# Loads of v paced by the planes of the running convolution, and an F32 context projection from unsplit weights

## Chip, cores and metric

The kernel runs on one core of one Trainium2 chip. The metric is the device time of one execution in microseconds (us), from the first to the last instruction and what lies around it; less is better.

## What is computed

One layer with two mixers that read the same normalised and modulated input: a chunked Mamba-2 scan in both directions, and an order-2 long convolution. Both matter here only in part. The first matter is the context prefix of 256 tokens, of which only the columns `m_xbc` (2048) and `m_dt` (32) of the input projection are wanted:

```python
h = rmsnorm(x, norm_w) * (1.0 + scale[:, None]) + shift[:, None]
hc = rmsnorm(ctx, norm_w) * (1.0 + scale_c) + shift_c
cols = in_projection(h, w_in, ALL_IN_NAMES)
cols_c = in_projection(hc, w_in, ("m_xbc", "m_dt"))
```

The second is the long convolution, order by order:

```python
u = depthwise_conv_centred(proj, conv_w, conv_b)
v, x1, x2 = jnp.split(u, 3, axis=-1)
z = v
for o, gate in enumerate((x1, x2)):
    z = gate * (bidir_long_conv(z, filt[:, 0, o], filt[:, 1, o]) + h_bias[o] * z)
```

Everything is float32. D_MODEL is 1024, SEQ 2048, CTX_LEN 256.

## The kernel before

The program is a row of phases, one block of instructions per engine each, with a barrier of all engines between them: modulation and filter network (`phase_modulation`), normalisation of the latent input together with the context projection (`phase_norm`), the input projection (`phase_in_projection`, the longest), filter taps, filter spectra, long convolutions (`phase_long_convs`), three phases of the scan, and the merge with the output projection. Each engine runs its own instructions in the order written; semaphores tie the engines together.

**`phase_norm`** (buffers `nl_...`). The 1024 channels are 8 tiles of 128 (KT). VectorE scales a piece of the input into PSUM (`scaled`, L435), ScalarE adds the shift and rounds to the high part (`high`, L389), VectorE makes the low part (`low`, L442). First come 8 pieces of the context (256 columns, `nl_c_hi` and `nl_c_lo`), then 32 pieces of the latent input (512 columns, `hl_hi` and `hl_lo`). Beside the 32 pieces run 17 tiles of weights of the context projection (16 of `m_xbc`, one of `m_dt`), two pieces to a tile. A tile of weights (128x1024, 512 KB) is loaded by SyncE (L324) into one of two slots, rounded to a high part by ScalarE (L396), its low part is made by GpSimd (L357), and TensorE then makes 24 matmuls of 256 columns (L370 to L372: high by high, high by low, low by high for each of 8 k). ScalarE evicts the result (L414), VectorE runs a three-tap convolution on it (`conv`, L451, L453, L456), ScalarE applies SiLU (L402), and SyncE stores it (L332). VectorE's order in an iteration n is: two pieces (scaled, low, scaled, low), then `conv(n - 1)`. ScalarE's is: eviction of tile n, rounding of weights n + 2, two `high`, SiLU of n - 1. A rounded tile is an `F32R` matmul operand, a plain one an `F32` operand; the `F32` matmuls of the long convolutions are the second kind.

**`phase_long_convs`** (buffers `conv_...`). The 1024 channels are four blocks of 256, each with two orders, so eight convolutions j in the order (block, order) = (0,0) (1,0) (0,1) (1,1) (2,0) (3,0) (2,1) (3,1). Convolution j has a stage of 16 steps q (`first` of j at L1005, `turn` and `last` of j - 1 at L1017 and L1027, the gate of j - 1 on VectorE at L1110), and then a stage of 32 planes (NPL): TensorE's `forward` (L1039), VectorE's product with the filter's spectrum (L1134, counted by the semaphore `s_p`), TensorE's two matmuls of `inverse` (L1049, L1050). SyncE loads the spectra, 512 KB for two planes, into four slots (SLOT, L948 and L950): the load of a slot waits until the two planes four slots earlier are multiplied. GpSimd's queue brings everything else by four 512 KB chunks each: v of a block (`load_x`, L960, into `x[:, blk % 2]`), the gate inputs of convolution j (`load_gate`, L967, three slots), and the stores of finished blocks (L979). GpSimd issues in program order: v of blocks 0 and 1 at the start; the gates of each convolution; and after the stores of block 0 (in j = 2) and block 1 (in j = 3) a wait for them to land, v of block 2 or 3, and the next gates.

Of the kernel before, what the change touches and what calls it, by code (L numbers as in the profile page):

```python
# [16 lines left out]
F32 = mybir.dt.float32  # L17
# [265 lines left out]
def phase_norm(nc, t, keep, rs, h_hi, h_lo, xbc_c, dt_c):  # L283
# [3 lines left out]
    with ExitStack() as ctx:  # L287
        ph = Phase(nc, "nl", ctx)
        c_hi, c_lo = ph.sb("c_hi", [P, KT, CTX], F32R), ph.sb("c_lo", [P, KT, CTX], F32R)
        x = ph.sb("x", [P, 4, 2, 512])  # L290
        w = ph.sb("w", [P, 2, D])
        w_hi, w_lo = ph.sb("w_hi", [P, 2, D], F32R), ph.sb("w_lo", [P, 2, D], F32R)
# [7 lines left out]
        s_w, s_whi, s_wlo, s_mm = ph.sems("w", 2), ph.sem("whi"), ph.sem("wlo"), ph.sem("mm")  # L300
# [11 lines left out]
        @block.sync  # L312
        def _(sp):
            def load_x(n):
                b, k, wd = piece(n)
                if n >= 4:
                    sp.wait_ge(s_xn, 2 * (n - 4) + 2)
                src = cv[:, k:k + 2, :] if b < 0 else xv[:, k:k + 2, b * 512:(b + 1) * 512]
                sp.dma_start(x[:, n % 4, :, 0:wd], src).then_inc(s_x[n % 4], 16)

            def load_w(n):
                if n >= 2:
                    sp.wait_ge(s_wlo, n - 1)
                sp.dma_start(w[:, n % 2, :], t["w_rec"][T_XBC + n]).then_inc(s_w[n % 2], 16)  # L324

            def store(n):
                if n < 2 * KT:
                    sp.wait_ge(s_res, n + 1)
                else:
                    sp.wait_ge(s_ev, NW)  # L330
                dst = xbc_c[n * P:(n + 1) * P, :] if n < 2 * KT else dt_c
                sp.dma_start(dst, res[:, n % 2, :]).then_inc(s_st[n % 2], 16)  # L332

            for n in range(4):
                load_x(n)
            sp.dma_start(taps[:], t["conv_taps"]).then_inc(s_taps, 16)
            load_w(0)
            load_w(1)
            nx = 4
            for n in range(NW):  # L340
                while nx < NX and nx < n + 8:
                    load_x(nx)
                    nx += 1
                if n + 2 < NW:
                    load_w(n + 2)
                if n >= 2:
                    store(n - 2)
            store(NW - 2)
            store(NW - 1)
            for q in range(2):  # L350
                sp.wait_ge(s_st[q], 16 * ((NW + 1 - q) // 2))

        @block.gpsimd
        def _(pool):
            for n in range(NW):
                pool.wait_ge(s_whi, n + 1)
                nc.gpsimd.tensor_tensor(w_lo[:, n % 2, :], w[:, n % 2, :], w_hi[:, n % 2, :].bitcast(F32),  # L357
                                        ALU.subtract).then_inc(s_wlo, 1)

        @block.tensor  # L360
        def _(pe):
            pe.wait_ge(s_lo, KT)
            for n in range(NW):
                pe.wait_ge(s_wlo, n + 1)
                if n >= 2:
                    pe.wait_ge(s_ev, n - 1)
                out = bank[n % 2][:, 0:CTX]
                for k in range(KT):
                    m = slice(k * P, (k + 1) * P)
                    pe.matmul(out, w_hi[:, n % 2, m], c_hi[:, k, :], start=(k == 0), stop=False)  # L370
                    pe.matmul(out, w_hi[:, n % 2, m], c_lo[:, k, :], start=False, stop=False)
                    mm = pe.matmul(out, w_lo[:, n % 2, m], c_hi[:, k, :], start=False, stop=(k == KT - 1))  # L372
                mm.then_inc(s_mm, 1)

        def place(n):

            b, k, wd = piece(n // 2)
            k += n % 2
            v = 1 if b < 0 else 0
            at = slice(0, CTX) if b < 0 else slice(b * 512, (b + 1) * 512)  # L380
            hi, lo = (c_hi, c_lo) if b < 0 else (h_hi, h_lo)
            return v, k, wd, hi[:, k, at], lo[:, k, at]

        @block.scalar
        def _(act):
# [6 lines left out]
            def weights(n):  # L392
                act.wait_ge(s_w[n % 2], 16 * (n // 2 + 1))
                if n >= 2:
                    act.wait_ge(s_mm, n - 1)
                nc.scalar.activation(w_hi[:, n % 2, :], w[:, n % 2, :], ACT.Copy).then_inc(s_whi, 1)  # L396

# [6 lines left out]
            for n in range(KT):  # L404
                high(n)
                if n in (4, 6):
                    weights(n // 2 - 2)
            done = KT
            for n in range(NW):
# [8 lines left out]
                if n + 2 < NW:  # L418
                    weights(n + 2)
# [8 lines left out]
        def _(dve):  # L428
            def scaled(n):
                v, k, wd, hi, lo = place(n)  # L430
                dve.wait_ge(s_x[n // 2 % 4], 16 * (n // 8 + 1))
                if n >= 2:
                    dve.wait_ge(s_lo, n - 1)
# [28 lines left out]
            scaled(0)  # L462
            for n in range(1, KT):
                scaled(n)
                low(n - 1)
            low(KT - 1)
# [13 lines left out]
            dve.wait_ge(s_lo, 2 * NX)  # L480
# [428 lines left out]
def phase_long_convs(nc, tables, u_s, z2_s, spec_s):  # L909

    NQ, NR, SLOT = 16, 8, 4
    with ExitStack() as ctx:
# [45 lines left out]
        def _(pool):  # L958
# [11 lines left out]
            for blk in range(2):  # L970
                for c in range(4):
                    load_x(blk, c)
            for j, (blk, o) in enumerate(convs):
                if o == 1:
# [6 lines left out]
                    if blk < 2:  # L981
                        pool.wait_ge(s_st, 64 * (blk + 1))
                        for c in range(4):
                            load_x(blk + 2, c)
# [1200 lines left out]
```

## Time and profile before

| What | us |
|---|---|
| Median of three runs | 4069.07 |
| Lowest and highest of them | 4060.92, 4069.66 |
| The profiled execution | 4071.49 |
| Span in its trace | 4069.7 |
| PE busy in the span | 3687.1 (91%) |
| DVE, ACT, POOL busy | 1726.3 (42%), 1215.7 (30%), 1023.3 (25%) |

All times in the trace are us from the start of the span of that one execution. PE is TensorE, DVE VectorE, ACT ScalarE, POOL GpSimd, SP SyncE; PEclk is the granted TensorE clock, 1.00 being 2.4 GHz and 0.50 being 1.2 GHz. An `F32` matmul is recorded as two matmuls, so a row of one `F32` matmul reads x2. An "idle before" in square brackets names what ended it. "q0 software_dynamic" is GpSimd's DMA queue, "q1" SyncE's.

### The profile page before, as it was taken

The numbers are of one execution on the slowest core, as the hardware profiler recorded it, in microseconds if no ns is written. First come the engines' busy times: TensorE is split into PE (matmuls) and PEld (weight loads), VectorE is DVE, ScalarE is ACT, GpSimd is POOL, SyncE is SP. The second block draws the span as 40 slices with busy tenths as digits, with TensorE's granted clock in tenths as the row PEclk, the third lists the DMA queues.
The fourth block names the chain that finished last, engine by engine and source line by source line (L and its number), as shares of the span: only waits on it lengthen the run. The fifth ranks groups of instructions, "written<-read, shape, count | busy, mean of one in ns | idle before, by whom it ended". The sixth has DMA issues, their size and how long they took to land. (4 is left out here: it accounts for less than half of the span.)

```text
span 4069.7 us, 44722 instructions
## 1 busy us (share of the span) xinstructions
PE 3687.1 (91%) x17082; PEld 2998.7 (74%) x17082; DVE 1726.3 (42%) x2050; ACT 1215.7 (30%) x2356; POOL 1023.3 (25%) x482
## 2 busy tenths in 40 slices
PE   5599999999999999996799899899766888799998
PEld 2578888888888888884599677677644777588886
DVE  5724430001433430003644454455367766566662
ACT  3411111111111011112377454455302554333332
POOL 0321112122222222111000101101047664344443
PEclk8899999999999999997899999999878999899999
DMA  6423322121211112116999757755667344555662
GB/s 250 159 86 119 114 96 77 62 77 62 77 62 77 67 72 77 62 67 246 306 301 275 179 135 165 166 130 125 157 241 275 125 156 135 209 190 194 207 191 101
DMA packets 386935, 597.40 MB, mean 147 GB/s; under 512 B 152019, under 2 KB 238979, under 8 KB 374395
## 3 DMA queue, kind: packets, MB, share of 16 engines
q1 hardware_dynamic: 297229, 403.94, 32.8%
q10 hardware_dynamic: 80336, 157.83, 10.1%
q0 software_dynamic: 9216, 33.56, 3.6%
q8 instruction: 99, 1.62, 0.2%
q14 instruction: 55, 0.45, 0.0%
HBM read 392.22 MB, written 203.03 MB: 146 GB/s over the span
## 5 line engine op out<-in xcount | busy, mean ns | idle before, releaser
L599 PE MATMUL pl_bank<-hl_hi,pl_w_hi 128*128 128x512 f32 x2336 | 923.7, 395 | 17.5 <-POOL pl_w_lo L570 17.5
L600 PE MATMUL pl_bank<-hl_lo,pl_w_hi 128*128 128x512 f32 x2336 | 922.6, 395 | 0.0
L601 PE MATMUL pl_bank<-hl_hi,pl_w_lo 128*128 128x512 f32 x2336 | 922.3, 395 | 0.0
L599 PEld LDWEIGHTS pl_bank<-hl_hi,pl_w_hi 128*128 128x128 f32 x2336 | 440.7, 189 | 120.0 <-issue 17.6
L601 PEld LDWEIGHTS pl_bank<-hl_hi,pl_w_lo 128*128 128x128 f32 x2336 | 440.7, 189 | 102.9
L600 PEld LDWEIGHTS pl_bank<-hl_lo,pl_w_hi 128*128 128x128 f32 x2336 | 440.7, 189 | 102.2
L567 POOL TENSOR_TENSOR pl_w_hi<-pl_w,pl_zero 128x1024 fp32r<-128x1024 f32 x73 | 138.1, 1892 | 1280.4 <-PE pl_bank L601 1275.7
L675 DVE TENSOR_SCALAR pl_res<-pl_raw,pl_taps 128x2048 f32<-128x2048 f32 x40 | 84.4, 2109 | 777.8 <-ACT pl_raw L625 777.8
L1775 PE MATMUL mo_bank<-mo_hi,mo_w_hi 128*128 128x512 f32 x768 | 305.5, 398 | 23.6 <-POOL mo_w_lo L1747 18.3
L1747 POOL TENSOR_TENSOR mo_w_lo<-mo_w,mo_w_hi 128x1024 fp32r<-128x1024 f32 x96 | 237.6, 2476 | 277.5 <-ACT mo_w_hi L1818 277.5
L1777 PE MATMUL mo_bank<-mo_hi,mo_w_lo 128*128 128x512 f32 x768 | 300.5, 391 | 0.0
L1776 PE MATMUL mo_bank<-mo_lo,mo_w_hi 128*128 128x512 f32 x768 | 300.4, 391 | 0.0
L625 ACT ACTIVATE pl_raw<-pl_bank 128x512 f32<-128x512 f32 x160 | 92.8, 598 | 664.3 <-PE pl_bank L601 430.0
L625 ACT ACTIVATE pl_res<-pl_bank 128x512 f32<-128x512 f32 x132 | 78.7, 598 | 617.8 <-PE pl_bank L601 617.2
L1134 DVE TENSOR_TENSOR conv_prod<-conv_bank,conv_spec 128x512 f32<-128x512 f32 x256 | 174.0, 690 | 179.9 <-PE conv_bank L1039 134.3
L1098 ACT COPY conv_v<-conv_bank 128x256 f32<-128x256 f32 x256 | 154.0, 602 | 243.2 <-PE conv_bank L1050 243.2
L570 POOL TENSOR_TENSOR pl_w_lo<-pl_w,pl_w_hi 128x1024 fp32r<-128x1024 f32 x73 | 199.3, 2730 | 5.8
L1775 PEld LDWEIGHTS mo_bank<-mo_hi,mo_w_hi 128*128 128x128 f32 x768 | 144.9, 189 | 59.1 <-issue 18.4
L1049 PE MATMUL conv_bank<-conv_prod,tab_wi 128*128 128x256 f32 x512 | 159.5, 394 | 24.4 <-DVE conv_prod L1134 23.7
L1776 PEld LDWEIGHTS mo_bank<-mo_lo,mo_w_hi 128*128 128x128 f32 x768 | 145.0, 189 | 30.9 <-issue 1.9
L1777 PEld LDWEIGHTS mo_bank<-mo_hi,mo_w_lo 128*128 128x128 f32 x768 | 145.0, 189 | 30.5
L967 POOL DMA_DIRECT2D conv_gin<-u_s x32 | 36.7, 1150 | 518.8 <-DVE conv_x L1110 512.0
(212 smaller groups left out, 5896.1 us busy)
## 6 DMA issues: line engine op xcount, KB each, us to landing
conv_spec<-spec_s SPq DMA_DIRECT2D x248, 256.0 KB, 4.9
mo_w<-in_w_br SPq DMA_DIRECT2D x96, 512.0 KB, 3.9
pl_w<-in_w_rec SPq DMA_DIRECT2D x73, 512.0 KB, 3.3
kern_s<-taps_res SPq DMA_DIRECT2D x16, 2048.0 KB, 7.0
spec_xin<-kern_s SPq DMA_DIRECT2D x64, 512.0 KB, 5.6
spec_s<-spec_res ACTq DMA_DIRECT2D x128, 256.0 KB, 4.1
st_xb<-tok_s SPq DMA_DIRECT2D x36, 768.0 KB, 7.0
u_s<-pl_res ACTq DMA_DIRECT2D x24, 1024.0 KB, 3.9
```

Of the source, the lines that this page charges most:

```text
L570: nc.gpsimd.tensor_tensor(w_lo[:, q, :], w[:, q, 0:D], w_hi[:, q, :].bitcast(F32), ALU.subtract).then_inc(s_lo, 1)
L599: pe.matmul(out, w_hi[:, q, m], h_hi[:, k, r], start=(k == 0), stop=False)
L600: pe.matmul(out, w_hi[:, q, m], h_lo[:, k, r], start=False, stop=False)
L601: mm = pe.matmul(out, w_lo[:, q, m], h_hi[:, k, r], start=False, stop=(k == KT - 1))
L625: nc.scalar.activation(dst, bank[b][:, 0:BW], func).then_inc(s_ev, 1)
L1049: pe.matmul(out, wi[:, k, :], prod[:, n % 4, 0, :], start=True, stop=False)
L1098: nc.scalar.copy(v[:, :, k], bank[2 + k % 2][:, 0:CB]).then_inc(s_vm, 1)
L1134: nc.vector.tensor_tensor(prod[:, n % 4], bank[ubank[k % 4]][:, None, 0:CB].to_broadcast([P, 2, CB]), spec[:, n // 2 % SLOT, :, k % 2], AL ...
L1747: nc.gpsimd.tensor_tensor(w_lo[:, s % 3, :], w[:, s % 3, :], w_hi[:, s % 3, :].bitcast(F32), ALU.subtract).then_inc(s_wlo, 1)
L1775: pe.matmul(bank[s % 4][:], w_hi[:, q, m], hi[:, slot, k, :], start=(k == 0), stop=False)
L1776: pe.matmul(bank[s % 4][:], w_hi[:, q, m], lo[:, slot, k, :], start=False, stop=False)
L1777: mm = pe.matmul(bank[s % 4][:], w_lo[:, q, m], hi[:, slot, k, :], start=False, stop=(k == KT - 1))
```

## The change

In `phase_norm` the context is kept as one F32 buffer `c` in place of `c_hi` and `c_lo`, and the weights are used as loaded: `w_hi` and `w_lo` go, `w` has four slots in place of two. The 24 F32R matmuls of a tile become 8 F32 matmuls. ScalarE's 17 roundings (L396), GpSimd's 17 subtractions (L357) and VectorE's 8 low parts of the context are gone. A tile's weights are loaded when the matmuls of four tiles earlier are done. The first group of matmuls waits for each piece of the context in turn and not for all eight. In `phase_long_convs`, v of block 1 is no longer loaded at the start but chunk by chunk during convolution 0, when its planes 4, 12, 20 and 28 are multiplied; v of blocks 2 and 3 are loaded likewise during convolutions 3 and 4. The number of bytes is the same.

```diff
@@ phase_norm
-        c_hi, c_lo = ph.sb("c_hi", [P, KT, CTX], F32R), ph.sb("c_lo", [P, KT, CTX], F32R)
+        c = ph.sb("c", [P, KT, CTX])
-        w = ph.sb("w", [P, 2, D])
-        w_hi, w_lo = ph.sb("w_hi", [P, 2, D], F32R), ph.sb("w_lo", [P, 2, D], F32R)
+        w = ph.sb("w", [P, 4, D])
...
             def load_w(n):
-                if n >= 2:
-                    sp.wait_ge(s_wlo, n - 1)
-                sp.dma_start(w[:, n % 2, :], t["w_rec"][T_XBC + n]).then_inc(s_w[n % 2], 16)
+                if n >= 4:
+                    sp.wait_ge(s_mm, n - 3)
+                sp.dma_start(w[:, n % 4, :], t["w_rec"][T_XBC + n]).then_inc(s_w[n % 4], 16)
...
-        @block.gpsimd
-        def _(pool):
-            for n in range(NW):
-                pool.wait_ge(s_whi, n + 1)
-                nc.gpsimd.tensor_tensor(w_lo[:, n % 2, :], w[:, n % 2, :], w_hi[:, n % 2, :].bitcast(F32),
-                                        ALU.subtract).then_inc(s_wlo, 1)
-
         @block.tensor
         def _(pe):
-            pe.wait_ge(s_lo, KT)
             for n in range(NW):
-                pe.wait_ge(s_wlo, n + 1)
+                pe.wait_ge(s_w[n % 4], 16 * (n // 4 + 1))
                 if n >= 2:
                     pe.wait_ge(s_ev, n - 1)
                 out = bank[n % 2][:, 0:CTX]
                 for k in range(KT):
-                    m = slice(k * P, (k + 1) * P)
-                    pe.matmul(out, w_hi[:, n % 2, m], c_hi[:, k, :], start=(k == 0), stop=False)
-                    pe.matmul(out, w_hi[:, n % 2, m], c_lo[:, k, :], start=False, stop=False)
-                    mm = pe.matmul(out, w_lo[:, n % 2, m], c_hi[:, k, :], start=False, stop=(k == KT - 1))
+                    if n == 0:
+                        pe.wait_ge(s_hi, k + 1)
+                    mm = pe.matmul(out, w[:, n % 4, k * P:(k + 1) * P], c[:, k, :], start=(k == 0), stop=(k == KT - 1))
                 mm.then_inc(s_mm, 1)
...
@@ phase_norm, VectorE
-            scaled(0)
-            for n in range(1, KT):
+            for n in range(KT):
                 scaled(n)
-                low(n - 1)
-            low(KT - 1)
@@ phase_long_convs, GpSimd's queue
-            for blk in range(2):
+            def load_paced(j, blk):
                 for c in range(4):
+                    pool.wait_ge(s_p, NPL * j + 8 * c + 4)
                     load_x(blk, c)
+
+            for c in range(4):
+                load_x(0, c)
             for j, (blk, o) in enumerate(convs):
+                if j == 0:
+                    load_paced(0, 1)
                 if o == 1:
                     for c in range(4):
                         load_gate(j, c)
...
                     if blk < 2:
                         pool.wait_ge(s_st, 64 * (blk + 1))
-                        for c in range(4):
-                            load_x(blk + 2, c)
+                        load_paced(j + 1, blk + 2)
```

GpSimd's queue in the long convolutions, from the start to the v of block 2. A wait is shown by the name under which the semaphore was first allocated: `ada_root` is the count of finished gates, `ada_rstd` that of stores, `ada_x1` that of planes, `s_p`; `z_s` is the buffer of finished blocks. Before:

```order
L960 DMA conv_x<-u_s 128x16x64 x8
L967 DMA conv_gin<-u_s 128x16x64 x3
L967 DMA conv_gin<-u_s 128x16x64 [waits ada_root] x9
L979 DMA z_s<-conv_x 128x16x64 [waits ada_root] x4
L960 DMA conv_x<-u_s 128x16x64 [waits ada_rstd]
L960 DMA conv_x<-u_s 128x16x64 x3
L967 DMA conv_gin<-u_s 128x16x64 [waits ada_root] x4
```

After:

```order
L940 DMA conv_x<-u_s 128x16x64 x4
L940 DMA conv_x<-u_s 128x16x64 [waits ada_x1] x4
L947 DMA conv_gin<-u_s 128x16x64 x3
L947 DMA conv_gin<-u_s 128x16x64 [waits ada_root] x9
L965 DMA z_s<-conv_x 128x16x64 [waits ada_root] x4
L940 DMA conv_x<-u_s 128x16x64 [waits ada_x1,ada_rstd]
L940 DMA conv_x<-u_s 128x16x64 [waits ada_x1] x3
L947 DMA conv_gin<-u_s 128x16x64 [waits ada_root] x4
```

Nothing is reordered, but each chunk of v of blocks 1, 2 and 3 now waits for planes, and the first gates behind it wait with it.

SyncE's queue at the start of `phase_norm` (`nl_x` pieces of context and latent input, `nl_w` weights, `nl_taps` convolution taps, `xbc_c` the result). Before:

```order
L336 DMA nl_taps<-in_conv_taps 128x160
L324 DMA nl_w<-in_w_rec 128x1024 x2
L319 DMA nl_x<-in_xT 128x2x512 x4
L324 DMA nl_w<-in_w_rec 128x1024
L319 DMA nl_x<-in_xT 128x2x512
L324 DMA nl_w<-in_w_rec 128x1024
```

After:

```order
L335 DMA nl_taps<-in_conv_taps 128x160
L323 DMA nl_w<-in_w_rec 128x1024 x4
L318 DMA nl_x<-in_xT 128x2x512 x5
L323 DMA nl_w<-in_w_rec 128x1024
L318 DMA nl_x<-in_xT 128x2x512
L323 DMA nl_w<-in_w_rec 128x1024
```

Two more tiles of weights (1 MB) go ahead of the first latent pieces.

ScalarE in `phase_norm`, from the first eviction on. Before:

```order
L414 ACTIVATE nl_raw<-nl_bank 128x256
L396 ACTIVATE nl_w_hi<-nl_w 128x1024
L389 ACTIVATE hl_hi<-nl_xn,keep_mod 128x512 x2
L414 ACTIVATE nl_raw<-nl_bank 128x256
L396 ACTIVATE nl_w_hi<-nl_w 128x1024
L389 ACTIVATE hl_hi<-nl_xn,keep_mod 128x512 x2
```

After:

```order
L397 ACTIVATE nl_raw<-nl_bank 128x256
L380 ACTIVATE hl_hi<-nl_xn,keep_mod 128x512 x2
L397 ACTIVATE nl_raw<-nl_bank 128x256
L380 ACTIVATE hl_hi<-nl_xn,keep_mod 128x512 x2
```

The rounding that stood between an eviction and the two `high` is gone, and with it its wait for the weights. VectorE's order in the latent part is unchanged.

## Rows read from the trace of the kernel before

**Rows 1.** Waits in `phase_norm`, 88 to 205: us in total, times, longest

```profile
PE nl_bank L370 <- POOL nl_w_lo L357: 29.5, 13, 4.3
DVE hl_lo L442 <- ACT hl_hi L389: 17.5, 11, 5.7
```

**Rows 2.** Timeline of `phase_norm`: start, duration, engine, line, what

```profile
90.67 1.06 ACT L396 ACTIVATE nl_w_hi<-nl_w 128x1024 fp32r<-128x1024 f32 x1 [1.80 <-DMA nl_w<-in_w_rec]
...
103.42 0.38 ACT L414 ACTIVATE nl_raw<-nl_bank 128x256 f32<-128x256 f32 x1 [0.38 <-PE nl_bank L372]
...
107.94 0.48 DVE L456 SCALAR_TENSOR_TENSOR nl_acc<-nl_raw,nl_taps,nl_acc 128x256 f32<-128x256 f32 x1
...
184.45 2.37 POOL L357 TENSOR_TENSOR nl_w_lo<-nl_w,nl_w_hi 128x1024 fp32r<-128x1024 f32 x1 [2.94 <-ACT nl_w_hi L396]
...
185.65 1.33 DVE L451 TENSOR_SCALAR nl_acc<-nl_raw,nl_taps 128x256 f32<-128x256 f32 x1
...
187.93 0.75 DVE L435 SCALAR_TENSOR_TENSOR nl_xn<-nl_x,keep_mod,rs_rows 128x512 f32<-128x512 f32 x1
...
190.77 0.40 DVE L451 TENSOR_SCALAR nl_acc<-nl_raw,nl_taps 128x256 f32<-128x256 f32 x1
...
192.13 0.75 DVE L442 SCALAR_TENSOR_TENSOR hl_lo<-nl_xn,keep_mod,hl_hi 128x512 fp32r<-128x512 f32 x1
```

**Rows 3.** Busy time by engine in a stretch, granted clock, DMA share, GB/s

```profile
125.00:145.00 20.00, 12.16 (x72) 11.46 (x72) 16.75 (x23) 9.41 (x17) 8.92 (x4) 0.83 0.60 189
```

**Rows 4.** Timeline of TensorE: F32R matmuls of `phase_norm`, F32 matmuls of the planes

```profile
121.20 0.28 PE L372 MATMUL nl_bank<-nl_c_hi,nl_w_lo 128*128 128x256 f32 x1
121.32 0.28 PE L370 MATMUL nl_bank<-nl_c_hi,nl_w_hi 128*128 128x256 f32 x1
...
2440.22 0.59 PE L1039 MATMUL conv_bank<-conv_y,tab_wf 128*128 128x256 f32 x2
2440.65 0.59 PE L1049 MATMUL conv_bank<-conv_prod,tab_wi 128*128 128x256 f32 x2
```

**Rows 5.** Timeline of VectorE in the first stage of convolution 0

```profile
2264.69 1.82 DVE L1072 COPY conv_y<-conv_bank 64x256 f32<-64x256 f32 x4 [0.33 <-PE conv_bank L1005]
2266.85 1.82 DVE L1072 COPY conv_y<-conv_bank 64x256 f32<-64x256 f32 x4 [0.33 <-PE conv_bank L1005]
```

**Rows 6.** The same stretch by engines, as Rows 3

```profile
2264.00:2268.00 4.00, 3.80 (x17) 2.42 (x16) 3.12 (x8) 2.62 (x8) 1.92 (x2) 1.00 1.06 237
```

**Rows 7.** Timeline of SyncE: first spectrum load in the planes of convolutions 2 to 5

```profile
2432.05 0.57 SPq L948 DMA_DIRECT2D conv_spec<-spec_s  x1
...
2508.62 0.57 SPq L948 DMA_DIRECT2D conv_spec<-spec_s  x1
...
2601.54 0.57 SPq L948 DMA_DIRECT2D conv_spec<-spec_s  x1
...
2694.52 0.57 SPq L948 DMA_DIRECT2D conv_spec<-spec_s  x1
```

**Rows 8.** Timeline of GpSimd's queue and VectorE in the planes of convolution 3

```profile
2513.66 4.58 POOL L960 DMA_DIRECT2D conv_x<-u_s  x4 [4.80 <-DMA z_s<-conv_x]
2518.23 3.43 POOL L967 DMA_DIRECT2D conv_gin<-u_s  x3
...
2530.17 1.29 DVE L1134 TENSOR_TENSOR conv_prod<-conv_bank,conv_spec 128x512 f32<-128x512 f32 x2 [6.88 <-DMA conv_spec<-spec_s]
```

**Rows 9.** Planes of convolutions 2 and 3 by engines, as Rows 3

```profile
2436.00:2462.00 26.00, 26.00 (x122) 22.89 (x121) 13.93 (x21) 12.05 (x20) 0.00 (x0) 1.00 0.94 224
2532.00:2546.00 14.00, 8.28 (x26) 6.01 (x25) 2.58 (x4) 2.36 (x4) 0.00 (x0) 0.74 1.05 233
```

**Rows 10.** GpSimd's DMA queue over the whole span: packets, MB, share of 16 engines

```profile
q0 software_dynamic: 9216, 33.56, 3.6%
```

**Rows 11.** From issue to landing: first loads and stores of `conv_x`, then `conv_spec`

```profile
DMA to landing us min/median/max: 4.8/7.8/20.3
...
DMA to landing us min/median/max: 3.5/4.9/22.9
```

**Rows 12.** Timeline of VectorE: first plane and first gate of convolution 0

```profile
2277.19 1.89 DVE L1134 TENSOR_TENSOR conv_prod<-conv_bank,conv_spec 128x512 f32<-128x512 f32 x3 [0.85 <-PE conv_bank L1039]
...
2325.99 0.69 DVE L1110 TENSOR_TENSOR conv_x<-conv_bank,conv_gin 128x512 f32<-128x512 f32 x1 [1.36 <-PE conv_bank L1027]
```

More of the change, by code:

```diff
@@ L299, in phase_norm @@
         s_x, s_xn, s_hi, s_lo = ph.sems("x", 4), ph.sem("xn_done"), ph.sem("hi"), ph.sem("lo")
-        s_w, s_whi, s_wlo, s_mm = ph.sems("w", 2), ph.sem("whi"), ph.sem("wlo"), ph.sem("mm")
+        s_w, s_mm = ph.sems("w", 4), ph.sem("mm")
         s_taps, s_edge, s_ev, s_tap, s_conv = ph.sem("taps_in"), ph.sem("edge"), ph.sem("ev"), ph.sem("tap"), ph.sem("conv")
@@ L336, in _ @@
             sp.dma_start(taps[:], t["conv_taps"]).then_inc(s_taps, 16)
-            load_w(0)
-            load_w(1)
+            for n in range(4):
+                load_w(n)
             nx = 4
@@ L343, in _ @@
                     nx += 1
-                if n + 2 < NW:
-                    load_w(n + 2)
+                if 1 <= n and n + 3 < NW:
+                    load_w(n + 3)
                 if n >= 2:
@@ L380, in place @@
             at = slice(0, CTX) if b < 0 else slice(b * 512, (b + 1) * 512)
-            hi, lo = (c_hi, c_lo) if b < 0 else (h_hi, h_lo)
-            return v, k, wd, hi[:, k, at], lo[:, k, at]
+            if b < 0:
+                return v, k, wd, c[:, k, :], None
+            return v, k, wd, h_hi[:, k, at], h_lo[:, k, at]
         @block.scalar
@@ L390, in high @@
                                      ).then_inc(s_hi, 1)
[L392 to L396, printed above, removed]
             def finish(n):
@@ L405, in _ @@
                 high(n)
-                if n in (4, 6):
-                    weights(n // 2 - 2)
             done = KT
@@ L417, in _ @@
                     nc.scalar.activation(res[:, n % 2, :], bank[n % 2][:, 0:CTX], ACT.Copy).then_inc(s_ev, 1)
-                if n + 2 < NW:
-                    weights(n + 2)
                 for _ in range(2):
@@ L431, in scaled @@
                 dve.wait_ge(s_x[n // 2 % 4], 16 * (n // 8 + 1))
-                if n >= 2:
-                    dve.wait_ge(s_lo, n - 1)
+                if n >= KT + 2:
+                    dve.wait_ge(s_lo, n - 1 - KT)
+                elif n >= 2:
+                    dve.wait_ge(s_hi, n - 1)
                 r = rs["ctx"][:] if v else rs["rows"][:, n // 8 - 1, :]
@@ L479, in _ @@
             conv(2 * KT - 1)
-            dve.wait_ge(s_lo, 2 * NX)
+            dve.wait_ge(s_lo, 2 * NX - KT)
 def phase_in_projection(nc, tag, w_rec, taps_d, groups, T, h_hi, h_lo, xbc_c, tok_s, ident_d):
```

## Prediction, made before the changed kernel ran

> **What bounds the kernel now.** I read the page first: TensorE is busy for 91% of the span, so I looked for the two phases of the diff and for what TensorE waits for in them. In `phase_norm` the table of waits shows TensorE waiting 29.5 us, 13 times, for GpSimd's low part of the weights, and VectorE 17.5 us for ScalarE's `high` [rows 1]. So neither TensorE nor one other engine is full there; a chain over load, rounding, subtraction and matmuls sets the pace, with VectorE close behind. The timeline gives the pace: the first `conv` ends at 107.94 + 0.48 = 108.4 and the last `low` of the phase starts at 192.13 [rows 2]; 14 iterations lie between, 83.7 us, 5.98 us each.
>
> In the long convolutions I looked at where each plane stage begins, by SyncE's first spectrum load in it. From convolution 2 to 3 it takes 76.57 us, from 3 to 4 92.92 and from 4 to 5 92.98 [rows 7]. The two long ones are 16.35 and 16.41 us longer for the same work. In the first of them GpSimd issues four chunks of v and three of gates in a row (seven of 512 KB), and VectorE then waits up to 6.88 us for a spectrum [rows 8]. The DMA engines are at a share of 1.05 there and the granted clock falls to 0.74, while an undisturbed stretch of planes runs at clock 1.00 with TensorE busy for all 26 us and the DMA share already 0.94 [rows 9]. The stage is bound by TensorE as long as the spectra come, and they leave little room for other transfers.
>
> **Part 1, context projection.** Removed from the path: ScalarE's rounding and GpSimd's subtraction. Weights are now four tiles ahead, so the load does not end last. What is next late is VectorE. Its iteration without waits is read between the `scaled` at 187.93 and the place four tile operations and one `conv` later, at 192.13: 4.20 us [rows 2]. That iteration had its first tap (L451) at 0.40 us. The one before had it at 1.33 us, ending just when GpSimd's 2.37 us subtraction, begun at 184.45, ends (186.8 against 187.0) [rows 2]. With GpSimd idle in the phase every first tap should be the short one. So VectorE's floor is 4.20 us an iteration.
>
> Is TensorE under it? F32 matmuls of 256 columns start 0.43 us apart in the planes at clock 1.00 [rows 4]; eight make 3.44 us. That is under 4.20, at 82% duty. Whether the clock stays up at that duty I read from the nearest case: in the first stage of convolution 0 four such matmuls (1.72 us) fall into each 2.16 us that VectorE takes [rows 5], 80% duty, and the clock there is 1.00 [rows 6]. With half the clock a tile would take 6.88 us and bind. ScalarE loses work. DMA: 0.60 of the engines at the present pace [rows 3] is 3.6 us of work in 5.98, which fits into 4.20 at a share of 0.86.
>
> The Trainium skill, page "FP8 and Floating Point Precision", section "TensorE Precision Notes", speaks against the edit: a true FP32 product is four passes through the array, where the split used three. At the 0.12 us of an F32R pass [rows 4] that would be 3.84 us a tile in place of 2.88, and the sum below would end about 0.4 us later for each of the two first tiles. The row of the F32 matmuls has 3.44 and I use it; either way VectorE's 4.20 covers it.
>
> The start: weights 0 are in place at 90.67 [rows 2]. The context's low parts no longer stand before it. The first tile, with TensorE cold, 8 x 0.86 = 6.9 us; the second 3.44; so it is ready at 101.0, against its eviction at 103.42 before [rows 2]. The first `conv` behind it has a first tap shorter by 0.9. I take 3.3 us. The two extra weight tiles ahead of the latent pieces are 1 MB that the first latent pieces wait behind; they are needed only when the first tile is evicted, so I cost that at nothing, and at up to 4 us if the first tile finds them missing. The 14 iterations give 14 x (5.98 - 4.20) = 24.9. The tail is the same. **Sum of part 1: 28.2 us**, bounds 18 (pace 4.9, if bursts of DMA or short spells of low clock show) and 31 (first tile warm).
>
> **Part 2, paced loads.** A chunk costs the DMA engines 3.6% of 4069.7 us by 64 transfers, 2.29 us [rows 10]. Eight planes at 3 x 0.43 us take 10.3 us [rows 4] and need four slots of spectra, 2.10 MB; at 224 / 0.94 = 238 GB/s [rows 9] that is 8.8 us. So one chunk in eight planes overloads by 2.29 - 1.5 = 0.8 us, four by 3.2. Against it stands the slack of the four slots: six planes, 7.7 us, less two issues (1.2 us) and 4.9 us of landing [rows 11], 1.6 us. I expect 1.6 us of waiting in each of the three paced stages, with bounds 0 (the fourth chunk, at plane 28, meets no urgent spectrum) and 3.5, and no fall of the clock, since each wait is short. In convolution 3 the store of block 0 still lands at 2513.66, after plane 4 [rows 8], so its first chunk starts where it did and the second follows after 7 us and not 10; that is in the bounds. The gates leave the plane stages and fall into the stages of 16 steps behind them.
>
> Gates are the wait that the change adds. In convolutions 0, 3 and 4 the first gate load now stands in GpSimd's queue behind plane 28. In convolution 0 that is 2277.19 + 28 x 1.29 = 2313.3, the chunk's issue takes 1.15, and a landing 7.8 us at the median [rows 11]: 2322.3. The first gate is used at 2325.99 [rows 12]. So it is hidden with 3.7 us to spare; who waits if not is VectorE's gate, behind it `first` of the next order. The start of convolution 0 I leave unchanged: chunk 0 of v is first in its queue in both kernels.
>
> Gain 16.35 + 16.41 = 32.8, cost 3 x 1.6 = 4.8. **Sum of part 2: 28.0 us**, bounds 22 and 33.
>
> The phases share nothing else, a barrier stands between them, and a phase that starts earlier runs alike. 4071.5 - 28.2 - 28.0 = 4015.3 for an execution like the profiled one, which lies 2.4 above the median of the runs: 4013.
>
> **Rivals.**
> (B) TensorE's clock does not stay up in the context projection. Then a tile takes 6.88 us and 14 iterations cost 14 x 2.68 = 37.5 more: 4050. For it: the clock is 0.83 there now [rows 3]. Against it: that is with idle stretches of up to 4.3 us [rows 1], and the 80% case runs at 1.00 [rows 6].
> (C) Pacing only spreads the cost: the DMA engines are the bound of the planes, every paced chunk costs its full 2.29 us, 12 of them 27.5 in place of 4.8. Time 4013 + 22.7 = 4036. For it: the share of 0.94 [rows 9]. Against: part of that share is the catching up after a gate load, and TensorE did not wait in it.
> (D) The gates come late. If the first takes the 20.3 us that is the longest landing [rows 11], it lands at 2334.7, 8.7 us late, in three stages 26 us: 4039. Against: that maximum belongs to eight loads in a row beside spectra, here there are two or three and the spectra of the next stage are nearly in.
> (E) Slower: each paced chunk makes TensorE wait long enough for its clock to fall, and the eight planes behind it run at 1.2 GHz, 10.3 us more each, 12 of them 124 us: 4137. It decides once 6 of the 12 chunks do this (56 us of gain by 10.3). For it: 0.74 in the burst [rows 9]. Against: that needed waits of many us in a row, with seven loads queued.
>
> **How the numbers follow.** Forecast 0.80, B 0.05, C 0.07, D 0.05, E 0.03. 0.2% is 8 us, about what a measurement of this kernel can tell from no change. The forecast's own bounds are 4013 + 10 + 6 = 4029 and 4013 - 3 - 5 = 4005; the runs before spread 8 us below their median, so I go down to 3999. Up to 4038 the range takes in C and most of D; B and E are out, with the far ends of the forecast. Faster: all but E and a remainder, 0.97; same 0.01; slower 0.02 (E is slower only from the sixth chunk on).
>
> **What will show it.** Part 1: the first taps near 0.40 us, TensorE's granted clock near 1.00 from the second tile on, VectorE idle for under 0.3 us an iteration, `phase_norm` ending near 166 and not 194. If instead VectorE waits for `hl_hi` each time and the clock is near 0.5, B. Part 2: four distances between plane stages near 77 to 79 us, VectorE's waits for spectra under 3 us each. If the waits add up to 9 us in a stage at clock 1.00, C; waits of the gate for `conv_gin`, D. I am wrong altogether if `phase_norm`'s iteration is not VectorE's, for instance if loads of x end last.

## Result and the profile after the change

| What | us |
|---|---|
| Changed kernel, median of four runs | 4012.8 |
| Lowest and highest of them | 4010.81, 4016.0 |
| Kernel before, beside it, median of four runs | 4067.88 |
| The profiled execution after | 4012.46 |
| Span in its trace | 4010.7 |

The ratio of the two is 0.9871 with a 95% interval of 0.9857 to 0.9884: the change saves 55 us. The prediction was 4013.0 us, with 3999 to 4038 as its range. The total is right to 0.2 us, which is better than its terms: some were off and cancelled. All readings below name lines of the changed kernel, where these lines stand 14 to 20 lines higher: `scaled` is L418, `low` L425, the taps are L434, L436 and L439, the eviction is L397 the product with the spectrum L1119, the loads of spectra L928 and L930, of v L940, of gates L947, and the stores L965.

**Context projection.** The timeline of VectorE, one iteration and the end of the phase (the last row is the first instruction of the next phase):

```profile
99.31 0.40 DVE L434 TENSOR_SCALAR nl_acc<-nl_raw,nl_taps 128x256 f32<-128x256 f32 x1
...
100.27 0.48 DVE L439 SCALAR_TENSOR_TENSOR nl_acc<-nl_raw,nl_taps,nl_acc 128x256 f32<-128x256 f32 x1
...
130.03 0.75 DVE L418 SCALAR_TENSOR_TENSOR nl_xn<-nl_x,keep_mod,rs_rows 128x512 f32<-128x512 f32 x1
...
134.22 0.75 DVE L418 SCALAR_TENSOR_TENSOR nl_xn<-nl_x,keep_mod,rs_rows 128x512 f32<-128x512 f32 x1
...
165.74 0.06 DVE L631 MEMSET pl_raw<- 128x1 f32 x1 [4.25 <-PEq L63]
```

From one `scaled` to the same one an iteration later it is 4.19 us, against 5.98 before [rows 2]. The waits of 80 to 180 say that nobody holds VectorE up any more (engine, line, what it waited for: us in total, times, longest):

```profile
ACT hl_hi L380 <- DVE nl_xn L418: 12.5, 16, 0.8
PE nl_bank L362 <- DMA nl_w<-in_w_rec: 9.7, 3, 9.0
DVE nl_xn L418 <- DMA nl_x<-in_xT: 6.2, 1, 6.2
```

ScalarE now waits for VectorE, where VectorE waited for ScalarE before [rows 1]. The DMA waits are those of the first tile: 9.0 of TensorE's 9.7 us, and all 6.2 of VectorE's. By engines (us of the stretch, busy us of PE, PEld, DVE, ACT, POOL, granted clock, DMA share, GB/s), to be laid beside [rows 3]:

```profile
105.00:125.00 20.00, 19.29 (x88) 16.23 (x87) 19.16 (x34) 10.19 (x20) 0.00 (x0) 1.00 0.87 284
125.00:145.00 20.00, 17.53 (x78) 13.96 (x77) 19.16 (x34) 9.61 (x20) 0.00 (x0) 1.00 0.88 281
```

VectorE is full (19.16 of 20 us), the granted clock is 1.00, and the DMA share rose from 0.60 to 0.88, since the same bytes pass in less time. The next phase begins at 165.74 and began at 198.50 before: 32.8 us. The first load of `phase_norm` is issued 0.9 us earlier in this execution than in the one before (80.67 against 81.57), so 31.9 of the 32.8 us are the phase's own.

**Long convolutions.** SyncE's first spectrum load in the planes of convolutions 3 to 6, as [rows 7]:

```profile
2477.11 0.57 SPq L928 DMA_DIRECT2D conv_spec<-spec_s  x1
...
2557.02 0.57 SPq L928 DMA_DIRECT2D conv_spec<-spec_s  x1
...
2636.25 0.57 SPq L928 DMA_DIRECT2D conv_spec<-spec_s  x1
...
2712.81 0.57 SPq L928 DMA_DIRECT2D conv_spec<-spec_s  x1
```

The stages take 79.91, 79.23 and 76.56 us; the first two were 92.92 and 92.98 before. Convolution 0, which has paced loads too, takes 78.88 where it took 76.98. From the first load of v to the last store the phase is 643.8 us long and was 669.5: 25.7 us. VectorE in the planes of convolution 3, and the same stretch by engines:

```profile
2498.42 1.29 DVE L1119 TENSOR_TENSOR conv_prod<-conv_bank,conv_spec 128x512 f32<-128x512 f32 x2 [1.47 <-PE conv_bank L1035]
2502.37 1.29 DVE L1119 TENSOR_TENSOR conv_prod<-conv_bank,conv_spec 128x512 f32<-128x512 f32 x2 [2.66 <-PE conv_bank L1024]
...
2512.80 1.29 DVE L1119 TENSOR_TENSOR conv_prod<-conv_bank,conv_spec 128x512 f32<-128x512 f32 x2 [3.68 <-PE conv_bank L1024]
```

```profile
2490.00:2500.00 10.00, 10.00 (x48) 8.79 (x47) 5.13 (x8) 4.51 (x8) 0.76 (x1) 1.00 1.06 227
2500.00:2510.00 10.00, 9.09 (x41) 7.38 (x40) 3.86 (x6) 3.93 (x7) 1.15 (x1) 1.00 1.05 237
2510.00:2520.00 10.00, 8.37 (x38) 6.82 (x38) 3.96 (x6) 4.14 (x7) 4.57 (x4) 1.00 1.05 225
```

The clock stays at 1.00, where the burst of before had 0.74 [rows 9], but the DMA engines are full (1.05) and from 2500 on, with the third chunk, TensorE has small gaps. The row at 2512.80 names TensorE's matmul, but that had ended at 2511.9. A load of a spectrum issued at 2503.68 took 8.8 us to land, to 2512.5, so it is the late spectrum that this product waited for. Over the whole phase the waits for transfers are:

```profile
DVE conv_prod L1119 <- DMA conv_spec<-spec_s: 16.9, 11, 4.1
...
DVE conv_x L1095 <- DMA conv_gin<-u_s: 7.2, 3, 2.8
```

The second row is the wait that the change added. The first does not count waits like the one at 2512.80, which the profile puts down to TensorE.

### The profile page after: what moved, and what is told of

The parts are those of the page before. It is cut to its first block and busy times, and to the rows that moved or that the text cites. A ratio compares the mean times of both kernels' runs of the same rounds, so it can differ in the third digit from the quotient of the medians.

```text
span 4010.7 us, 44395 instructions
## 1 busy us (share of the span) xinstructions
PE 3676.8 (92%) x16946; PEld 2984.5 (74%) x16946; DVE 1705.7 (43%) x2042; ACT 1201.0 (30%) x2339; POOL 982.8 (25%) x465
## 5 line engine op out<-in xcount | busy, mean ns | idle before, releaser
L1119 DVE TENSOR_TENSOR conv_prod<-conv_bank,conv_spec 128x512 f32<-128x512 f32 x256 | 172.8, 689 | 156.3 <-PE conv_bank L1024 115.0
```

The costliest lines, as they stand in the source:

```text
L1119: nc.vector.tensor_tensor(prod[:, n % 4], bank[ubank[k % 4]][:, None, 0:CB].to_broadcast([P, 2, CB]), spec[:, n // 2 % SLOT, :, k % 2], AL ...
```

## The experiments

Each kernel is the changed one with the edit shown, unless said otherwise; `...` marks lines that are left out. Times are medians of four runs (of two for e3 and e4), ratios go against the kernel before. "Phase end" is the start of `phase_in_projection` in the trace (165.74 above), "excess" is a stage's distance over 76.57.

### The two parts alone

```diff
# e1_projection_only: after, but
-def phase_long_convs  (after)
+def phase_long_convs  (before)
# e2_paced_only: before, but
-def phase_long_convs  (before)
+def phase_long_convs  (after)
```

> The changed kernel with the long convolutions of before (v loaded unpaced). Theory: the two parts are independent, and part 1 is worth what its phase is shorter in the trace of after, 32.8 us, so about 4035 (33 below before), with phase_norm ending as in after and the plane stages of convolutions 3 and 4 16 us too long as in before. Rival: part of the 55 us exists only with both parts together (a start of the convolutions at another moment, a clock state carried along); then this kernel and the one with part 2 alone do not add up to 55.

> The kernel before with the paced loads of v alone. Theory: part 2 is worth 25.7 us (the convolutions in the trace of after are that much shorter), so about 4042, not the 28.0 of the prediction: VectorE's waits for spectra leave 8.4 us in the three paced stages and not 4.8. Rival: part 2 is worth 28 or more and the rest is lost elsewhere.

The projection alone: 4039.32 us, ratio 0.9929 (0.9913 to 0.9946), phase end 166.60, so 31.9 us gained there; its convolutions still have the two long stages, 92.53 and 92.28. The paced loads alone: 4043.07 us, ratio 0.9948 (0.9932 to 0.9965), convolutions 642.7 us long, 26.8 less. In the traces the parts give 31.9 and 26.8, close to the 32.8 and 25.7 of the whole. By the medians they give 26 and 22, some 7 us less than the 55 of both; each interval is 7 us to either side, so a coupling is neither shown nor excluded.

The traces also show how much the same code varies from one execution to the next. The convolutions of the first kernel are those of before, and take 673.1 us where they took 669.5: the excess of convolution 0 is 4.1 and was 0.4, and the last convolution takes 85.1 and took 82.2. In the six kernels whose convolutions are those of the change (e2, the changed kernel, and e3, e4, e9 and e10 below, which alter the projection alone) the three excesses add up to 5.9 to 10.8 us, and a single one lies between 0.0 and 5.5. A difference of 2 or 3 us between two single traces says nothing here.

### What the projection gains from: GpSimd's absence, the count of matmuls, VectorE's work, the slots

```diff
# e3_gpsimd_back
                 if n >= 4:
                     sp.wait_ge(s_mm, n - 3)
+                    sp.wait_ge(s_spare, n - 3)
...
+            for n in range(NW):
+                pool.wait_ge(s_w[n % 4], 16 * (n // 4 + 1))
+                pool.wait_ge(s_lo, max(1, min(2 * n + 1, 2 * NX - KT)))
...
+                nc.gpsimd.tensor_tensor(spare[:], w[:, n % 4, :], w[:, n % 4, :], ALU.subtract).then_inc(s_spare, 1)
```

The 17 subtractions are back, but nobody on the path uses their result; only the reload of a slot of weights waits for it, and TensorE waits for no weights in that kernel's iterations.

> The changed kernel with 17 GpSimd subtractions of 128x1024 put back into phase_norm, off the chain: they read the weights and write a buffer that nobody reads, started while VectorE makes the first low part of an iteration. Theory: VectorE's first tap (L434's like) and GpSimd's instruction exclude each other, so the tap takes about 1.3 us again where they meet and not 0.40, an iteration 5.1 and not 4.20, 14 us in all: about 4027. Rival: the 1.3 us came from ScalarE's rounding or from the DMA traffic of before, not from GpSimd; then the taps stay at 0.40 and the time at 4013.

Measured: 4036.28 us, ratio 0.9928, phase end 189.49, the iteration 5.70 us. The prediction's reading, that the first tap is long while GpSimd subtracts, would make that tap 1.3 us. It stays at 0.40 to 0.41 in all 16 places; the second one is long. VectorE and GpSimd in that kernel (L446, L448 and L451 are its three taps):

```profile
122.12 0.41 DVE L446 TENSOR_SCALAR nl_acc<-nl_raw,nl_taps 128x256 f32<-128x256 f32 x1
122.56 2.00 DVE L448 SCALAR_TENSOR_TENSOR nl_acc<-nl_raw,nl_taps,nl_acc 128x256 f32<-128x256 f32 x1
124.59 0.49 DVE L451 SCALAR_TENSOR_TENSOR nl_acc<-nl_raw,nl_taps,nl_acc 128x256 f32<-128x256 f32 x1
```

```profile
122.34 1.94 POOL L362 TENSOR_TENSOR nl_spare<-nl_w 128x1024 fp32r<-128x1024 f32 x1 [3.77 <-DVE hl_lo L437]
```

GpSimd ends at 124.28, VectorE's tap at 124.56. So the mechanism is confirmed, and wider than I had it: the second tap, with two inputs in SBUF and begun while GpSimd works, lasts until GpSimd is done, in each of the 16 places. Which tap is hit depends on where GpSimd's start falls. Here it costs 1.5 us in each iteration, not the 0.9 that I had expected for a first tap. In this kernel the subtractions that are off the path cost 24 of the 33 us that the projection gained. In the kernel before they held 14 first taps for 0.8 to 0.9 us each, 12.5 us in all, and TensorE waited for their results besides; how the gain divides among the links that were taken away is not shown, since the split form was not run with four slots or without GpSimd.

```diff
# e4_twelve_matmuls
+                for k in range(4):
...
+                    pe.matmul(out, w[:, n % 4, k * P:(k + 1) * P], c[:, k, :], start=True, stop=True)
                 for k in range(KT):
```

> The changed kernel with 12 F32 matmuls for a tile in phase_norm in place of 8; the four more are overwritten, so the output is the same. Theory: VectorE sets the pace at 4.20 us and TensorE has 0.76 us to spare at 3.44; with 12 x 0.43 = 5.16 us TensorE sets it, an iteration costs 0.96 to 1.0 more, 15 us in all: about 4028, at a clock of 1.00. Rival B of the prediction (the clock does not hold): 12 x 0.86 = 10.3 us, 6 us an iteration, about 4105. Rival C, TensorE is far from the bound: no change.

The four more are overwritten by the eight that follow. Measured: 4025.67 us, ratio 0.9902, phase end 182.42. The iteration is 5.18 us, which is 12 x 0.43, and TensorE has no gap left:

```profile
105.00:125.00 20.00, 20.00 (x95) 17.60 (x94) 15.80 (x28) 7.83 (x16) 0.00 (x0) 1.00 0.68 216
```

So eight F32 matmuls are 3.44 us, as [rows 4] had it, and leave VectorE's 4.20 as the bound.

```diff
# e9_tap_on_scalar
@@ ScalarE, at the eviction
+                    nc.scalar.activation(acc[:, n % 2, :], bank[n % 2][:, 0:CTX], ACT.Identity,
+                                         scale=taps[:, n * NTAP + 1:n * NTAP + 2], bias=taps[:, n * NTAP + 3:n * NTAP + 4]).then_inc(s_a0, 1)
...
@@ VectorE
-                nc.vector.tensor_scalar(acc[:, q, :], raw[:, q, 1:CTX + 1], w1, bias, ALU.mult, ALU.add).then_inc(s_tap, 1)
```

> The changed kernel with the first tap of the convolution (0.40 us on VectorE, the multiply and add that starts the sum) moved to ScalarE, which reads it from the same bank as its eviction. Theory (VectorE alone sets the iteration of the projection, 4.20 us, and TensorE needs 3.44): the iteration falls by the tap to about 3.8 us, the phase ends 15 x 0.4 = 6 us earlier, about 4007 us. Rival 1 (the weights' loads, 512 KB an iteration at a DMA share already of 0.87 to 0.88, become the bound as soon as the iteration is shorter): the share goes to about 0.97 and the iteration stays at 4.0 us or more, a gain under 3 us. Rival 2 (ScalarE's second read of the bank keeps TensorE waiting): new waits of TensorE for ScalarE of over 0.5 us an iteration, no gain.

Measured: 4004.6 us (3999.58 to 4009.47), ratio 0.9845 (0.9828 to 0.9861), phase end 161.69. The iteration is 3.75 us, 13 times in a row after a first one of 3.85, the DMA share 0.90:

```profile
105.00:125.00 20.00, 20.00 (x94) 17.61 (x93) 19.27 (x34) 13.28 (x26) 0.00 (x0) 1.00 0.90 298
```

VectorE alone set 4.20: taking 0.44 us from it takes 0.44 from the iteration. Neither the loads nor ScalarE's second read of the bank stand in the way. The phase as a whole ends only 4.1 us earlier: the first `conv` ended 2.1 us later in this execution. Its first matmul began 0.9 us later than in the changed kernel, and its first tile took 7.0 us to its eviction and not 5.2, at a granted clock of 0.50 until 94 where the other had 1.00 from 92.

```diff
# e10_two_weight_slots
-        w = ph.sb("w", [P, 4, D])
+        w = ph.sb("w", [P, 2, D])
...
-                if n >= 4:
-                    sp.wait_ge(s_mm, n - 3)
+                if n >= 2:
+                    sp.wait_ge(s_mm, n - 1)
...
```

> The changed kernel with two slots for the projection's weights in place of four: a load is issued only when the matmuls of the iteration two earlier are done. Theory (a load takes about 6.2 us from issue to landing in this phase): a slot's period is a load and the 3.44 us of its matmuls, (6.2 + 3.44) / 2 = 4.8 us an iteration in place of 4.20, 14 to 16 iterations, +8 to +10 us, about 4022 us, with waits of TensorE for the weights of about 1 us each. Rival (a load that has the engines to itself lands sooner, 3 to 5 us): the period stays at 4.20 to 4.3, no change, 4013 us: the four slots bring nothing.

Measured: 4024.79 us, ratio 0.9894 (0.9878 to 0.9911), phase end 179.03, 13.3 us later. Tiles of TensorE in that kernel:

```profile
117.05 3.72 PE L362 MATMUL nl_bank<-nl_c,nl_w 128*128 128x256 f32 x16 [2.72 <-DMA nl_w<-in_w_rec]
121.82 3.72 PE L362 MATMUL nl_bank<-nl_c,nl_w 128*128 128x256 f32 x16 [1.05 <-DMA nl_w<-in_w_rec]
127.26 3.72 PE L362 MATMUL nl_bank<-nl_c,nl_w 128*128 128x256 f32 x16 [1.72 <-DMA nl_w<-in_w_rec]
```

TensorE waits for weights 12 times, the first tile's wait included, and the iterations are 5.03 us long in the mean, from 4.19 to 7.45. The theory had 4.8: a load issued at 120.85 is used at 127.26, after 6.4 us, near its 6.2 (from issue to landing alone the loads of this kernel take 5.1 at the median; the rest was not traced). So unsplit weights need more than two slots: with two, 13 of the 33 us go back. Three were not tried.

### What the paced loads cost and why

```diff
# e5_paced_by_four
-                    pool.wait_ge(s_p, NPL * j + 8 * c + 4)
+                    pool.wait_ge(s_p, NPL * j + 4 * c + 4)
```

> The changed kernel with the chunks of v paced by planes 4, 8, 12, 16 in place of 4, 12, 20, 28. Theory (overload against the slack of the four spectrum slots): four planes take 5.2 us and their spectra 4.4 us of all DMA engines, so 0.8 is left for a chunk of 2.29 and each overloads by 1.5 us, four by 6.1, against 3.2 with eight planes. The paced stages of convolutions 0, 3 and 4, which are 2.3, 3.3 and 2.7 us too long in the trace of after, should each be 3 us longer: about 4022. Rival: only the bytes in the stage count, not their spacing; then 4013 as before.

Measured: 4038.32 us, ratio 0.9929 (0.9912 to 0.9945), excess 11.8, 12.3 and 13.0. Added up this is 37.1 us, more than the 33.2 of the kernel before, which had 0.4 in convolution 0, and the convolutions take 670.9 us against 669.5. The kernel without any pacing, e1, has 4039.32 us: this pacing is worth nothing. I had expected 3 us more a stage and counted four chunks. GpSimd's queue in the planes of convolution 3 shows seven loads between 2487.59 and 2507.1, the gates as well; the last five of them:

```profile
2494.91 1.15 POOL L940 DMA_DIRECT2D conv_x<-u_s  x1 [4.01 <-DVE conv_prod L1119]
2502.56 1.15 POOL L940 DMA_DIRECT2D conv_x<-u_s  x1 [6.50 <-DVE conv_prod L1119]
2503.70 3.43 POOL L947 DMA_DIRECT2D conv_gin<-u_s  x3
```

With the last chunk at plane 16 its gates follow at once into planes that still need spectra; the distance of eight keeps the gates out of the planes. That this is most of its worth is my reading: no run changes the distance with the gates held back.

```diff
# e6_two_chunks_late
                 for c in range(4):
-                    pool.wait_ge(s_p, NPL * j + 8 * c + 4)
-                    load_x(blk, c)
+                    if c < 2:
+                        pool.wait_ge(s_p, NPL * j + (4, 16)[c])
+                        load_x(blk, c)
+                    else:
+                        pool.wait_ge(s_p, NPL * j + 28)
+                        load_gate(j, c - 2)
+                for c in range(2, 4):
+                    load_x(blk, c)
...
```

> The changed kernel with two chunks of v at planes 4 and 16, then the first two gates at plane 28, then the last two chunks of v, which land in the stage of 16 steps where the DMA engines have room. The bytes are the same. Theory: two chunks overload by less than the slots' slack, the first gate is no longer behind a chunk of v: the 8.3 us left in the three stages go to under 2 and the 7.2 us in which VectorE waits for gate inputs go too, about 4005. Rival: the last chunks, now 10 us later, are missing in steps 8 to 15, and the time stays at 4013 or more.

Measured: 4008.95 us (4005.3 to 4012.11), ratio 0.9855 (0.9838 to 0.9871), excess 1.4, 1.5 and 1.9 instead of 2.3, 3.3 and 2.7, and no gate waits for its load. The sum of 4.8 lies below the 5.9 to 10.8 of the six kernels with the pacing of the change. The time points below the changed kernel's too, but the ranges (to 4012.11, from 4010.81) and the intervals overlap: that it is faster is not shown.

```diff
# e7_eight_slots; e8_unpaced_eight_slots: the same line, with phase_long_convs of before
-    NQ, NR, SLOT = 16, 8, 4
+    NQ, NR, SLOT = 16, 8, 8
```

> The changed kernel with eight spectrum slots in place of four, nothing else. Theory: the slack grows by eight planes, 10.3 us, far above the overload of a stage, so VectorE no longer waits for spectra in paced stages and each takes 76.6 us: about 4005. Rival: the DMA engines' bandwidth over the whole stage is the bound, more slots only shift it: 4013.

> The long convolutions of before, v unpaced, with eight slots, and the changed context projection. Theory: the burst of seven loads delays the spectra by 16 us, the four more slots cover 10.3 of it, so the two long stages are 6 us too long and not 16.4: about 4017 where four slots unpaced gave 4039. Rival: the queues share the DMA engines so that the spectra starve whatever is buffered, and it stays at 4039; or the slack covers all and it is 4005, then pacing was never needed.

Measured: 3998.7 us (3994.32 to 4002.22), ratio 0.9833 (0.9816 to 0.9849) with pacing, 4006.56 us (4004.19 to 4008.29), ratio 0.9853 (0.9837 to 0.987) without. With pacing and eight slots, every stage takes 76.56 or 76.57 us and no engine waits for a spectrum, though the DMA engines are as full as with four slots:

```profile
2490.00:2500.00 10.00, 10.00 (x48) 8.81 (x47) 5.17 (x9) 4.82 (x8) 1.15 (x1) 1.00 1.06 230
2500.00:2510.00 10.00, 10.00 (x48) 8.81 (x47) 5.22 (x8) 4.61 (x8) 2.65 (x3) 1.00 1.05 229
```

Compare the same stretches of the changed kernel above: 9.09 there, 10.00 here. Without pacing the excess is 5.6 and 2.5 us, a third and a sixth of the 16.4 of before. So the burst of seven loads does not cost its transfer time; it costs what the prefetch cannot bridge. In these stages eight slots without pacing (8.1 us) come out like pacing with four slots (8.3 us). That the kernel is still faster than the changed one, 4006.56 against 4012.8 us, lies for the most part in the last convolution.

With pacing and eight slots the phase became 12.9 us shorter, and the three excesses explain only 8.3. The rest is in the last convolution, which neither I nor the change had looked at. GpSimd's queue and VectorE there, in the changed kernel:

```profile
2788.46 1.16 POOL L965 DMA_DIRECT2D z_s<-conv_x  x1 [4.88 <-DVE conv_x L1095]
2789.61 3.44 POOL L947 DMA_DIRECT2D conv_gin<-u_s  x3
```

```profile
2800.34 1.29 DVE L1119 TENSOR_TENSOR conv_prod<-conv_bank,conv_spec 128x512 f32<-128x512 f32 x2 [4.05 <-DMA conv_spec<-spec_s]
2806.11 1.29 DVE L1119 TENSOR_TENSOR conv_prod<-conv_bank,conv_spec 128x512 f32<-128x512 f32 x2 [4.49 <-issue]
```

A store and three gate loads go out as the planes begin, and the planes wait. From the last product of convolution 6 to that of convolution 7 it is 82.2 us in the kernel before, 81.7 in the changed one and 76.6 with eight slots, paced or not. That it is these four transfers that make the spectra late is read from their times; no run moves them.

### The best together

```diff
# e11_eight_slots_tap: the edits of e9 and e7
# e12_eight_slots_tap_late: the edits of e9, e7 and e6
```

> Two edits that each stood alone: eight slots for the spectra in place of four (3998.7 us) and the first tap on ScalarE. Theory: they lie in different phases and add, 3998.7 - 6 = 3993 us. Rival: with the weights' loads as the bound of the projection the tap gives under 3 us, 3996 to 3999 us.

> As the run with eight slots and the tap on ScalarE, with the loads in another order: two x chunks at planes 4 and 16, then two gate loads at plane 28, then the last two x chunks. Theory: with eight slots no matmul waits for a spectrum any more, and of the waits of the long convolutions only those of the gates for their own loads are left (9.1 us in three places); gates that are asked for four planes earlier land in time, 3993 - 9 = 3984 us at most, if all three waits lie on the chain. Rival: the last x chunks, now behind the gates, land late for the next stage, and what the gates gain the first transforms lose: 3993 us or more.

Measured: 3990.33 us (3987.52 to 3991.63), ratio 0.981 (0.9794 to 0.9827), and 3991.62 us, ratio 0.9817 (0.9801 to 0.9833). The two edits add: the tap gives 8 us with either number of slots. The third gives nothing, and that settles the question of the gates with eight slots. The first of the two kernels has this row among its waits in the long convolutions, the second has no such row:

```profile
DVE conv_x L1100 <- DMA conv_gin<-u_s: 8.0, 3, 3.3
```

Yet all stages are 76.57 or 76.58 us in both and the phase is 630.4 us long in both. These 8 us are not on the chain that sets the end.

## Why the prediction was right, point by point

**Bound of the projection.** Right, and shown from both sides: VectorE's 4.20 us was forecast from one iteration without waits [rows 2] and the trace has 4.19; less work on VectorE shortens it (e9), more on TensorE takes over at 12 x 0.43 (e4). The 14 iterations gave 14 x 1.79 = 25.1 us against 24.9. Rival B is out: the granted clock is 1.00 in them.

**The start of the projection was mis-sized:** 3.3 us forecast, 7.7 measured (the first `conv` ends at 100.75, 108.4 before). I let the first tile start when weights 0 landed before [rows 2], at 90.67, with TensorE cold for a whole tile, 6.9 us. In the trace the matmuls start at 88.80 and the first eviction is at 93.99, 5.2 us later; the second is at 97.44, 3.5 behind it, where I had 101.0. TensorE was cold for the first half of the tile only (clock in the seventh number, as in [rows 3]):

```profile
88.00:90.00 2.00, 1.21 (x3) 1.03 (x4) 0.00 (x0) 0.45 (x2) 0.00 (x0) 0.50 1.02 414
92.00:94.00 2.00, 2.00 (x11) 1.75 (x10) 0.00 (x0) 0.01 (x1) 0.00 (x0) 1.00 1.05 396
```

With 25.1 this makes the 32.8 us. It lies above my bound of 31 (31.6 by its own terms), which stood for the case "first tile warm". Of the 1.9 us by which the first weights land earlier, 0.9 is the earlier start of the phase; the other 1.0 was not traced. Nor was the second eviction what the first `conv` waited for. The first latent piece landed only at 94.11, and from there VectorE worked without a pause of over 0.1 us up to the `conv`. So the two extra tiles of weights ahead of it, which I had at nothing, did cost something, but little: ScalarE, done with the first eviction, waited 0.5 us for VectorE's `scaled` of that piece. How long the first tile stays at the low clock varies: 7.0 us to its eviction in e9, all of it but the end at 0.50, as I had assumed.

**First taps.** That with GpSimd idle every first tap would be the short one was right (403 ns in the mean of 16), its reason half right: it is not the first tap as such that GpSimd stretches, but the tap that begins while it works (e3, and [rows 2] for the first tap).

**Waits of the paced stages were mis-sized:** 1.6 us each forecast, 2.3, 3.3 and 2.7 measured, inside the bounds of 0 to 3.5. In other executions of the same convolutions the bound does not hold: 4.5 and 3.8 in e10, 5.5 in e4. The term that was mis-sized is the slack of 1.6 us, from a landing of 4.9 us for the spectra. From 2480 to 2520, in the planes of convolution 3, loads of spectra take 5.2 to 16.3 us to land, 9.1 at the median, which leaves no slack; the overload of 3.2 us alone would then be the wait, an estimate from my own terms. The gaps come from the third chunk on, not with the fourth at plane 28. That the slack of the slots is what counts was right, and eight of them take the excess to zero (e7). Rival C would have had 27.5 us of cost for 12 chunks; 8.3 were measured, and at most 10.8 in another execution. Rival E is out: the clock is 1.00 throughout the paced planes.

**Gates.** Wrong in the number, harmless in the end. I had the first gate of convolution 0 hidden with 3.7 us to spare, from a landing of 7.8. The trace has the loads issued at 2282.54 and the gate at 2294.63, after 12 us and a wait of 1.6, and 2.8 in the other two stages. So rival D's mechanism occurred. Its price did not. In the changed kernel itself, from the last product of a plane stage to the first of the next it is 36.9, 37.3 and 37.3 us behind the three paced stages, where the gates waited, and 37.3 behind an undisturbed one. With eight slots and the waits taken away the time is the same (e11, e12).

**Sum.** Part 1 gave 32.8 in place of 28.2, part 2 25.7 in place of 28.0. The three stages cost 3.5 more than I had; against it convolution 0 had an excess of 0.4 before, and the start and the last convolution came out 0.8 shorter. That is 2.3 more in all, with 0.5 more in phases that the change does not touch, and the profiled execution lies 0.3 under the median, where I had taken 2.4 above. These differences cancel in the 0.2 us by which the forecast missed: that it is so near is luck, the more so as the same kernel's runs lie up to 5 us apart. What I did not see is that the same four slots also cost 5 us in the last convolution, before as after.

## What to carry to other kernels

Where full DMA engines meet a stage that is bound by TensorE, the cost of a burst is what the prefetch cannot bridge: look first whether there is room for more slots (here worth 14 us on top of the pacing, 5 of them in a stage that the pacing did not touch), and only then spread the burst, with what stands behind it in the queue counted too. An engine whose result nobody waits for can still cost its neighbour time: in e3 GpSimd's subtractions cost 24 us by their mere presence. Before you remove a wait that the table of waits shows, ask whether the stage distance moves with it.

## What was not expected of the hardware

A tap of VectorE and a subtraction of GpSimd excluded each other for a whole instruction. With GpSimd at work from 122.34 to 124.28 in e3, VectorE's tap with two SBUF inputs took 2.00 us instead of 0.48. In the kernel before it was the first tap, with one input and its output in SBUF, that was held from 185.65 to 186.98 while GpSimd ran from 184.45 to 186.82 [rows 2]. The `low` begun under the same subtraction kept its time:

```profile
184.98 0.75 DVE L442 SCALAR_TENSOR_TENSOR hl_lo<-nl_xn,keep_mod,hl_hi 128x512 fp32r<-128x512 f32 x1
```

A `scaled` begun at 103.35, under a subtraction from 101.96 to 104.35, took 0.76 us. Both have one of their two tensor inputs in PSUM. The Trainium skill, page "SBUF — State Buffer", section "SBUF: two separate sides", has this as an exclusive lock on a shared pair of ports, held for a whole instruction, which a VectorE instruction needs that runs in a two-port mode, or that has two SBUF inputs while GpSimd reads SBUF, as the subtraction does. Rows and rule agree, also in that a 0.41 us tap that began before GpSimd kept its time. For the first tap of the kernel before the rule asks for a two-port mode; no row shows in which mode it ran.

DMA engines at a share of 1.05 did not lower TensorE's speed in itself: in the planes of convolution 3 with eight slots, from 2480 to 2520, it was busy for all 40 us at granted clock 1.00, and the stage took the same 76.57 us as the others.
